# Gated-delta heads of a two-block transformer kernel: convolution steps of one pass, the second turned block in the outputs' PSUM bank, decay products behind level 0's copies

## The reference, cut to what matters

```python
def first_block(x, ...):                         # 1024 positions, 1024 columns
    h = _rmsnorm(x, ln_mix_pre[l])
    proj = jnp.einsum('bsd,dc->bsc', h, w_in[l])
    qkv = silu(conv_general_dilated(proj[..., C_QA:C_ZA], conv_w, ...))   # 5 taps per column
    qa, ka = l2norm of q and k by head; va; decay g and beta, forward and backward
    o_a = _chunk_gated_delta(qa, ka, va, g_f, beta_f) + flip(_chunk_gated_delta(flip ...))
    o_a = _rmsnorm(o_a, norm_a[l]) * jax.nn.silu(z)
    ...                                          # dilated attention, gates, feed-forward
def _chunk_gated_delta(q, k, v, g, beta):        # chunks; here of 128 rows in the kernel
    sol = triangular_solve(a_kk + eye, rhs, unit_diagonal=True)
    a_qk = einsum(q, k) * gam                    # "outputs' decay products"
    ...                                          # scan over chunks: state, outputs
def reference(...):
    x = first_block(...)
    return second_block(x, ...)                  # differential attention and an LRU
```

## Time and profile before

| what | us |
|---|---|
| median of 3 runs (3649.76 to 3652.07) | 3651.28 |
| the profiled execution's own time | 3642.13 |
| its span, first to last instruction | 3640.3 |
| PE busy in it | 3405.5 |
| mean granted PE clock | 0.975 of full speed |

### The profile page before, as it was taken

The page is one execution under the profiler, slowest core; times in us unless marked ns, Lnnn a source line. Parts: engine busy times, 40 slices in busy tenths (PEclk is TensorE's granted clock), DMA queues, the critical chain, the costliest instruction groups (busy, mean ns, idle before and its releaser), DMA issues.

```text
span 3640.3 us, 36888 instructions
## 1 busy us (share of the span) xinstructions
PE 3405.5 (94%) x15359; PEld 2427.8 (67%) x15359; DVE 1395.5 (38%) x2006; ACT 963.1 (26%) x2228; POOL 358.8 (10%) x433
## 2 busy tenths in 40 slices
PE   8999989988888999999999999999999997998997
PEld 5555655655656556585674478777777785777776
DVE  3444444455444201101012334444444466632452
ACT  3333232333333102202121023111111133312452
POOL 0211222222222100000001000000000011100111
PEclk9999999999999999999999999999999998998998
DMA  3111010101001011101124232111111140101000
GB/s 138 58 47 41 24 52 32 38 24 35 24 25 41 34 55 41 38 15 58 35 108 180 77 123 73 52 47 47 47 47 47 47 146 25 47 24 53 36 30 29
DMA packets 55526, 194.72 MB, mean 53 GB/s; under 512 B 7200, under 2 KB 14880, under 8 KB 42304
## 3 DMA queue, kind: packets, MB, share of 16 engines
q1 hardware_dynamic: 54496, 191.29, 14.9%
q10 hardware_dynamic: 864, 1.09, 0.1%
HBM read 158.37 MB, written 33.98 MB: 53 GB/s over the span
## 4 chain that ended last, share of the span: by engine, by line
PE 82%; DVE 9%; ACT 6%; issue 1%; POOL 1%; DMA 1%; SPq 0%; ACTq 0%; POOLq 0%; DVEq 0%
PE ps L543 14%; PE ps L1408 10%; PE ps L2028 9%; PE ps L2029 9%; PE ps L2030 9%; PE ps L1433 6%; PE ps L1729 4%; PE ps L1905 3%; PE ps L610 3%; PE ps L616 3%; DVE ar L985 2%; PE ps L2897 1%; PE ps L1483 1%; DVE r L2021 1%; ACT r L2016 1%
## 5 line engine op out<-in xcount | busy, mean ns | idle before, releaser
L543 PE MATMUL ps<-ar 128*128 128x512 f32 x1408 | 673.7, 606 | 27.4 <-ACT ps L747 19.5
L2028 PE MATMUL ps<-r,r 128*128 128x512 f32 (+3 forms) x1296 | 479.2, 370 | 17.5 <-DVE ar L2554 4.7
L2029 PE MATMUL ps<-r,r 128*128 128x512 f32 (+3 forms) x1296 | 463.6, 358 | 0.0
L2030 PE MATMUL ps<-r,r 128*128 128x512 f32 (+3 forms) x1296 | 462.9, 357 | 0.0
L543 PEld LDWEIGHTS ps<-ar 128*128 128x128 f32 x1408 | 250.0, 195 | 231.2 <-issue 213.0
L1408 PE MATMUL ps<-ar 128*128 128x512 f32 x896 | 398.3, 594 | 0.3 <-ACT ar L762 0.3
L2028 PEld LDWEIGHTS ps<-r,r 128*128 128x128 f32 (+1 forms) x1296 | 253.8, 196 | 60.4 <-issue 6.6
L1408 PEld LDWEIGHTS ps<-ar 128*128 128x128 f32 x896 | 166.0, 191 | 180.8 <-issue 180.2
L2029 PEld LDWEIGHTS ps<-r,r 128*128 128x128 f32 (+1 forms) x1296 | 253.6, 196 | 39.4 <-issue 6.6
L2030 PEld LDWEIGHTS ps<-r,r 128*128 128x128 f32 (+1 forms) x1296 | 252.7, 195 | 34.3
L2028 PE MATMUL ps<-r 128*128 128x512 f32 x512 | 201.3, 393 | 20.0 <-DVE ar L2278 17.8
(11 more groups left out here) (311 smaller groups left out, 4613.3 us busy)
## 6 DMA issues: line engine op xcount, KB each, us to landing
ar<-wst SPq DMA_DIRECT2D x102, 1024.0 KB, 4.9
ar<-x SPq DMA_DIRECT2D x16, 512.0 KB, 11.7
ar<-sc_g SPq DMA_DIRECT2D x32, 256.0 KB, 5.1
sc_h<-ar SPq DMA_DIRECT2D x32, 256.0 KB, 2.0
sc_x<-ar SPq DMA_DIRECT2D x16, 512.0 KB, 3.2
ar<-sc_x SPq DMA_DIRECT2D x16, 512.0 KB, 4.2
sc_b<-ar SPq DMA_DIRECT2D x24, 260.0 KB, 2.0
ar<-sc_b SPq DMA_DIRECT2D x3, 2080.0 KB, 20.2
```

The lines of the kernel that those rows point to most:

```text
L543: o = t.do.matmul(bk, wv[:, kt, c:c + 128], hT[:, kt, 512 * hf:512 * hf + 512], start=(kt == 0), stop=(kt == 7))
L2028: t.do.matmul(o, l[0], r[0], start=first, stop=False)
L2029: t.do.matmul(o, l[0], r[1], start=False, stop=False)
L2030: return t.do.matmul(o, l[1], r[0], start=False, stop=last)
```

## The change

Six edits, all within the GDN heads; no instruction is added or taken away, but for the six waits that follow from the new order.

1. Each of the four passes of a convolution (L985 before, L996 after) has a step of its own; before two of them shared one. The tanh on ACT, the product on DVE and the first turned block on PE stand one to three prep steps later; the second turned block keeps its place at the end of the half.
2. The second turned block goes to bank 5 (`pe_bank5`), which the outputs' transposes use; not for head 0.
3. `aq` (L1049 before, L1066 after) stands behind level 0's masked copies instead of ahead of them; PE's XT of level 1 now waits for it, since it overwrites bank 3.
4. ACT takes the tanh of q, k and v later, behind the next half's copy.
5. DVE's idle steps are fewer, to make up for the added ones.
6. The fin thread has the share 0.0 to 0.42 of a stage instead of 0.05 to 0.5.

```diff
-        inv_dve = flow(... for n in ["MT", "aq", ("XT", 0), ("X", 0)] + L3(("XT", "X"))])
+        inv_dve = flow(... for n in ["MT", ("XT", 0), ("X", 0), "aq"] + L3(("XT", "X"))])
...
-                threads.append((("fin", (s - 3) // 2), NFIN, 0.05, 0.5))
+                threads.append((("fin", (s - 3) // 2), NFIN, 0.0, 0.42))
...
+        held5 = []
+
+        def pe_bank5(t, f, key):
+            if held5:
+                t.wait_ge(*held5.pop())
+            held5.append((f, key))
+            place_of[f.name, key] = 5
+            return bank(5)
...
+            if hf and h:
+                bk = pe_bank5(t, prep_ev, (h, s, hf))
+            else:
+                bk = pe_bank(t, prep_ev, (h, s, hf))
...
-                if n in (5, 7):
-                    pe_flip(t, h, "fq", (n - 5) // 2, chq[h % 2])
+                if n in (6, 7):
+                    pe_flip(t, h, "fq", n - 6, chq[h % 2])
...
-                t.wait_ge(inv_dve, k(("XT", n - 1)))
+                t.wait_ge(inv_dve, k(("XT", n - 1) if n > 1 else "aq"))
...
-            yield from idle(2)
-            act_tanh(a, h, "q")
-            yield
+            yield from idle(3)
             if h:
                 a.wait_ge(conv_sum, (h - 1, "k"))
             act_part(a, h, "k", 0, raw[1][:, 2:1026])
+            yield
+            act_tanh(a, h, "q")
             yield
...
                 o.then_inc(*(dve_step.tick() if j < 4 else conv_sum.tick((h, c))))
-                if j in (1, 3):
-                    yield
+                yield
             yield
...
-            yield from idle(4)
+            yield from idle(2)
...
+            v.wait_ge(masks, 0)
+            v.wait_ge(inv_act, k("ident"))
+            v.wait_ge(inv_dve, k("MT"))
+            v.do.copy_predicated(mixed1(BT), blocked1(mk[:, 0, :]), blocked1(MT)).then_inc(*inv_dve.tick(k(("XT", 0))))
+            v.wait_ge(inv_mm, k("M"))
+            v.do.copy_predicated(mixed1(FB0), blocked1(mk[:, 0, :]), blocked1(bank(4))).then_inc(*inv_dve.tick(k(("X", 0))))
             if h >= 2 - part:
                 v.wait_ge(scan_mm, (h - 2 + part, 7, "o"))
...
```

More of the change, by code:

```diff
@@ L393, in program @@
         inv_mm = flow("inv_mm", [(*c, n) for c in hp for n in ["kq", "M"] + L3(("Y", "XT", "X"))])
-        inv_dve = flow("inv_dve", [(*c, n) for c in hp for n in ["MT", "aq", ("XT", 0), ("X", 0)] + L3(("XT", "X"))])
+        inv_dve = flow("inv_dve", [(*c, n) for c in hp for n in ["MT", ("XT", 0), ("X", 0), "aq"] + L3(("XT", "X"))])
         steps8 = [(h, n) for h in heads for n in range(8)]
@@ L550, in pe_flip @@
             t.wait_ge(conv_out, (h, s[1]))
-            bk = pe_bank(t, prep_ev, (h, s, hf))
+            if hf and h:
+                bk = pe_bank5(t, prep_ev, (h, s, hf))
+            else:
+                bk = pe_bank(t, prep_ev, (h, s, hf))
             for j in range(4):
@@ L569, in pe_prep1 @@
                 for n, _ in enumerate(pe_proj(t, h, s)):
-                    if n in (FK if f == "fk" else (5, 7)):
-                        pe_flip(t, h, f, (n - 5) // 2, src)
+                    if n in (6, 7):
+                        pe_flip(t, h, f, n - 6, src)
                     yield
-        FK = (5, 7)
         def pe_fill(t, h):
@@ L670, in pe_fin @@
             for hf in range(2):
-                if hf or h:
-                    t.wait_ge(fin_z, fins[2 * h + hf - 1])
+                bk = pe_bank5(t, fin_z, (h, hf))
                 for j in range(4):
-                    o = t.do.transpose(q4(bank(5), j), q4(oc[h % 2], 4 * hf + j), ident)
+                    o = t.do.transpose(q4(bk, j), q4(oc[h % 2], 4 * hf + j), ident)
                 o.then_inc(*fin_mm.tick((h, hf)))
@@ L806, in act_prep1 @@
             q = h % 2
-            yield from idle(2)
-            act_tanh(a, h, "k")
-            yield
+            yield from idle(3)
             if h in GATES:
-                for hf in range(2):
-                    act_gate(a, h, "g1", hf)
-                    yield
-                    yield from idle(3)
+                act_gate(a, h, "g1", 0)
+                yield
+                act_tanh(a, h, "k")
+                yield from idle(3)
+                act_gate(a, h, "g1", 1)
+                yield
+                yield from idle(3)
             a.wait_ge(conv_sum, (h, "q"))
             act_part(a, h, "v", 0, raw[0][:, 2:1026])
+            yield
+            if h not in GATES:
+                act_tanh(a, h, "k")
             yield
@@ L828, in act_prep1 @@
             yield
-            yield from idle(2)
-            act_tanh(a, h, "v")
-            yield
+            yield from idle(3)
             if h >= 2:
@@ L834, in act_prep1 @@
             act_part(a, h, "z", 0, zt[q], 0.5)
+            yield
+            act_tanh(a, h, "v")
             yield
@@ L1009, in dve_prep1 @@
             yield from conv_steps(v, h, "k", chk[q])
-            yield from idle(12 if h in GATES else 4)
+            yield from idle(10 if h in GATES else 2)
             for n, _ in enumerate(conv_steps(v, h, "v", vf)):
@@ L1050, in dve_inv @@
             o.then_inc(*inv_dve.tick(k("aq")))
-            yield
-            v.wait_ge(masks, 0)
-            v.wait_ge(inv_act, k("ident"))
-            v.wait_ge(inv_dve, k("MT"))
-            v.do.copy_predicated(mixed1(BT), blocked1(mk[:, 0, :]), blocked1(MT)).then_inc(*inv_dve.tick(k(("XT", 0))))
-            v.wait_ge(inv_mm, k("M"))
-            v.do.copy_predicated(mixed1(FB0), blocked1(mk[:, 0, :]), blocked1(bank(4))).then_inc(*inv_dve.tick(k(("X", 0))))
             yield
```

## The result

The changed kernel takes 3614.18 us (median of 4 runs, 3609.74 to 3615.27), the kernel before 3651.42 us beside it (3649.76 to 3652.07). The ratio is 0.9896, 95% interval 0.9879 to 0.9914: 37 us or 1.0% faster. The forecast was 3638.7 us, the range 3626 to 3651. The sign was right; the gain is three times the forecast.

The account below looks back on a forecast made before the run. PE was taken to bound the kernel, so only its 113 us of standing still in the GDN heads could shrink; gains in waits and clock less costs of later starts summed to -12.6 us: 3651.3 - 12.6 = 3638.7, range 3626 to 3651.

Parts of the forecast that it names:

- near 8: Sign that the forecast is right: in stage 11 the wait for `MT`'s turn is near 8 us.
- (c): Behind v's block: the 0.93 us wait goes, but scan product L647 still waits for DVE's L1083; credit 0.
- blocks and passes: GDN heads: bank 5 -7.4, one pass per step -9.1 and -7.15, later first block +6.15, head 0 +0.5 us.
- later turned block: Ungated stages: first turned block a step later makes copies by ACT late, 1.7 or 0.35 us per stage: +6.15 us.
- starts of the odd stages: Level 1's Y with fin ahead of GpSimd's sum: stages 9, 11, 13 +7.5, 15 +2.5, 3, 5, 7 +0.9, 1 -2.0 us.
- Clock: Stages 9, 11, 13: slow matmuls fall before Y's wait, -4.5 us; further -1.7 in seven stages at level 4's Y not taken.
- The base: Durations came from one execution of 3642.1 us; the sum was taken off the runs' median, 3651.3 us, 9 us higher.
- Fin on POOL lands whole: Rival: in seven stages fin's delay of the sum L1160/L1170 reaches level 1's Y, all of 5.1 us: 3663 us; 10%.
- Freed waits return: Rival: half of the credit behind k's block and of the pass terms returns at the next copy: 3650 us; 20%.
- The anchors don't hold: Rival: ACT is free earlier, so (a) adds ten us and (c) 7 to the gain: 3622 us; 8%.
- (a): Behind q's block: PE would start its units 1.47 us sooner, but then meets the turn of `MT`; credit 0.
- The rule weighed there: Stages 3, 5, 7: two-input VectorE and GpSimd instructions on SBUF exclude each other wholly; Y +1.0 instead of +0.3 us.

Follow-up runs that it names:

- e17: Kernel before plus two additional 128x512 products only in PE's waits behind the copy of X (level 5 in stages 1 to 7, level 4 in 8 to 13): 3641.2 us.
- e10: The kernel before, unchanged, profiled a second time: 3650.5 us; the first profiled execution took 3642.1 us.
- e9: Kernel before with one-pass convolution steps and ACT's tanh moved, but PE's turned blocks at their old steps 5 and 7: 3615.3 us.
- e1: Changed kernel with the fin thread's share put back to 0.05 to 0.5: 3587.6 us.
- e8: Changed kernel with one more yield, putting GpSimd's sum ahead of fin's power and scaling again, fin early everywhere else: 3592.9 us.
- e13: e1 plus two additional 128x512 products in the waits for `MT` (stages 9, 11, 13) and for w (once per head): 3573.3 us.
- e2: Kernel before with only the second turned block given to bank 5: 3634.5 us.
- e12: Changed kernel plus 4, 8 or 5 additional 128x512 products in PE's wait for `MT` in the odd stages from 3 on: 3613.6 us.

## Why the forecast fell short

**The order and the waits.** Stage 11, in us, from the timelines of both kernels (before to after):

| stretch | before | after | moved | forecast |
|---|---|---|---|---|
| XT of level 6 to turn of MT | 13.28 | 18.17 | +4.89 | +5.1 |
| turn to level 1's Y | 6.37 | 3.59 | -2.78 | -2.6 |
| to level 2's Y | 9.09 | 7.43 | -1.66 | -1.5 |
| to level 3's Y | 7.44 | 8.87 | +1.43 | +1.35 |
| to level 4's Y | 10.05 | 7.48 | -2.57 | -2.35 |
| to level 5's Y | 10.49 | 8.82 | -1.67 | 0 |
| to XT of level 6 | 9.24 | 9.47 | +0.23 | +0.35 |

Six of seven steps came within 0.3 us. What the prediction named as signs came too: no waits of projections outside head 0, the turn's wait 7.98 ("near 8"), Y behind the copy of X 0.77, X of level 2 1.58, w 1.92 (so (c) paid nothing).

**The whole sum, term by term.** The same reckoning over all stages, in us, from the starts of the turn, of each level's Y and of level 6's XT, against the execution that the prediction used:

| term | forecast | measured |
|---|---|---|
| blocks and passes, with the later turned block | -17.0 | -25.0 |
| starts of the odd stages, up to level 1's Y | +8.9 | +8.2 |
| clock behind level 1's Y in stages 9, 11, 13 | -4.5 | -3.7 |
| clock behind Y of level 4 (9, 11, 13) and 5 (3, 5, 7) | 0 | -10.0 |
| lowered stretches elsewhere | 0 | +2.5 |
| sum | -12.6 | -28.0 |
| second execution of before instead of the first | 0 | -8.3 |
| sum against the second execution | -12.6 | -36.3 |

**The step that failed is "Clock".** It gave -4.5, and of the bound "a further -1.7 in seven stages where the shortened wait before Y of level 4 no longer lowers the clock" it said "I take none of the latter". That is the one row of stage 11 that missed, and it came in stages 3, 5, 7, 9, 11 and 13 (in the gated ones behind level 5's Y): six times 1.7, about 10 us. e17 shows that such clock can be had without shortening a wait. It did not all stay: two new lowered stretches on the way to the turn in stages 10 and 14 cost 3.1 us, and one behind level 1's Y in stage 15 cost 1.0, while one ahead of stage 0 is missing (-1.6). That is why the busy time lost to the clock fell by only 2.1 us against this execution.

**The base hid almost as much again.** "No wait worked with scales with that, so I take the sum off the median" was right about waits (e10) and wrong in what it left out. The profiled execution had about 9 us less of lowered clock in this stretch than the second one, which stands where the median does. The changed kernel, with 19.3 us, lost less to the clock than either.

**The blocks and passes were sized too small**, by 8.0 us, 6.8 of them in stages 0 to 7. In stages 3, 5 and 7 the waits of 1.09 and 1.94 us went whole and gave 3.5 us: their own 3.0 and about a quarter of a us for each stop, where 1.05 and 1.3 were credited. The prediction put the cost around a stop at nothing.

**The starts** came right as a sum, with errors that cancel. In stages 3, 5 and 7 level 1's Y came 0.6, 0.9 and 0.2 us sooner, counted from level 6's XT, where +0.3 was taken; in stages 9 and 13 it came 2.8 us later and in stage 11 2.1, where +2.5 was taken. Stage 15 went the other way: Y +4.0 instead of +2.5, since turn, unit and Y all ran at a lowered clock.

```profile
1134.43 1.12 PE L614 MATMUL ps<-ar 128*128 128x128 f32 x4 [6.31 <-DVE ar L1052]
1135.34 3.62 PE L552 MATMUL ps<-ar 128*128 128x512 f32 x4
1138.75 1.91 PE L621 MATMUL ps<-ar 128*128 128x128 f32 x8
```

That is the timeline of the changed kernel in stage 15; the window around it has a granted clock of 0.63:

```profile
1128.00:1142.00 14.00, 7.69 (x21) 0.63 0.05 20
```

**The later turned block** was +6.15. Its rows came as said (+1.43 in the table). As a price it was put wrongly: e9 shows that the old step would now cost more.

**The rivals.** "Fin on POOL lands whole" did not happen against the kernel before: of the 5.1 us at the turn 2.1 to 2.8 reached level 1's Y in stages 9, 11 and 13. But e1 and e8 show that fin's early share costs 26.5 us, and its order on GpSimd 21.3, beside the other five edits. The prediction had only the sum of the starts and did not see how much of it was fin's. "Freed waits return" did not happen: the halved terms gave more than was credited. "The anchors don't hold" gave a time nearer the result (3622), but not by its reason, since (a) and (c) paid nothing in the changed kernel.

**The rule weighed there.** In stage 5 the power started at 457.24 beside two passes (2.60 us together) and took 2.64 us, and the scaling began behind both:

```profile
457.08 2.60 DVE L996 SCALAR_TENSOR_TENSOR ar<-ar 128x1024 f32<-128x1024 f32 x2
457.24 2.64 POOL L1195 TENSOR_TENSOR ar<-ar 128x8 f32<-128x8 f32 x1 [1.45 <-DVE ar L1121]
...
459.96 1.89 POOL L1198 TENSOR_TENSOR ar<-ar 128x1024 f32<-128x1024 f32 x1
```

The Trainium skill, "SBUF — State Buffer", section "Who interferes with whom", says that such a pair contends for shared ports which one engine holds at a time. This trace agrees in part: the two passes kept their length and the power took 2.64 us instead of 1.67, but it ended 0.2 us behind the passes and did not have to run as a whole behind them. So the price by that rule, +1.0 at level 1's Y, did not come. Counted from level 6's XT, power and scaling ended at 14.0 and 16.0 us and the turn came at 18.1; the prediction has 14.1, 16.0 and 18.3 without the rule, and 19.6 for the turn with it.

**Left open.** Which waits lower the clock in a given execution is not settled: the places differ between two executions of one kernel, and in e17 some were new, so what the clock gave can be told only in sum. Behind the heads e1 and e13 have the same 10268 rows of PE, and PE is busy 2318.7 and 2313.0 us in them; what makes the difference was not looked into.

## What to carry to other kernels

Where PE is nine tenths busy with many waits of 1 to 4 us, price each wait three times: its own length, the quarter of a us that a stop costs around it here, and the work behind it if the granted clock is lowered there. When two executions of one kernel have the same waits and differ in busy time, that difference belongs in the sum, and the profiled execution may be the lucky one. Edits of one stretch are not to be added up: four of them gave 17, 40, 16 and 0 us alone and 37 together, because one edit's cost was covered by a wait that the others removed; and because waits freed by one edit return at the next anchor (e2). So run the change without each of its parts too: without fin's edit (e1) it is 26.5 us faster than the whole.

## What the hardware showed that I had not expected

- Two executions of the same kernel, with waits equal to 0.1 us per line, differed by 8.5 us in how long PE was busy with the same products.
- Work put into a wait for its own sake can make a kernel faster: with 17.2 us of additional products e17 is 8.6 us faster than the kernel before, and e13 has 7.2 us less in the stages than e1. In e12, with 35.3 us of them, nothing was gained.
- A stop of PE costs about 0.16 us ahead of it and 0.1 us behind it besides its length, so the changed kernel is busy 8 us less at the same clock.
- A 128x512 f32 product is two rows of the trace and takes 0.86 us; I had counted 0.43 us.
- GpSimd's 128x8 power took 2.64 us beside DVE's passes and 1.67 us alone; a masked copy from and to SBUF took 2.98 us beside the scaling (e1, stage 11) and 1.29 alone.
